# Moving the second block's activation tiles to other start addresses in SBUF

## What is computed

```python
hn = rms_norm(h, norm_mix_g)
u, gb_in, gc_in, v_in, ga_lin, gbr_lin = split(hn @ w_in)        # each 2048 wide
pooled = causal_multiscale_pool(u)                               # trailing means over 2, 4, 8, 16 tokens
y_a = einsum("blgc,gcd->blgd", pooled, pool_w) * pool_scale      # four 512 x 512 products
y_b = (gb_in * causal_depthwise_conv(gc_in * v_in, conv_w)) @ conv_out_w
g_a, g_b = split(sigmoid(concat(ga_lin, gbr_lin) + b_gate))
h = h + (g_a * y_a + g_b * y_b) @ w_o
hn = rms_norm(h, norm_ffn_g)
gate, up = split(hn @ w_gate_up)                                 # 2 x 5632 wide
h = h + (silu(gate) * up) @ w_down
out = rms_norm(h, norm_final_g)[:, 16:]
```

## Time and profile before

| | before |
|---|---|
| runs | 3424.66, 3426.06, 3426.75 us |
| profiled execution | 3418.24 us, span 3416.9 us |
| TensorE busy | 3285.0 us, 96% of the span |
| DVE, ACT, POOL busy | 48%, 40%, 5% |
| mean granted TensorE clock | 0.979 of full speed |
| second block | about 1893 to 3417 us of the span |
| moved from and to HBM | 566 MB, 166 GB/s on average |

### The profile page before, as it was taken

The page is one execution under the profiler, slowest core; times in us unless marked ns, Lnnn a source line. Parts: engine busy times, 40 slices in busy tenths (PEclk is TensorE's granted clock), DMA queues, the critical chain, the costliest instruction groups (busy, mean ns, idle before and its releaser), DMA issues.

```text
span 3416.9 us, 52152 instructions
## 1 busy us (share of the span) xinstructions
PE 3285.0 (96%) x21958; PEld 2848.6 (83%) x21958; DVE 1654.4 (48%) x2688; ACT 1360.5 (40%) x2179; POOL 173.0 (5%) x252
## 2 busy tenths in 40 slices
PE   6899999978999999999899999999999999999998
PEld 2588888863458879887459999999999999999998
DVE  1322233364663353355585675565555654555444
ACT  2322232344442254333454443344444444444343
POOL 3001000011001101000201000000000000000000
PEclk8999999989999989999899999999999999999999
DMA  8633222227644256433425455555555455555554
GB/s 308 246 123 120 93 93 97 80 76 257 237 170 154 93 185 204 142 130 115 157 77 200 160 180 185 185 179 191 186 186 188 168 187 185 187 189 186 186 187 153
DMA packets 152826, 566.09 MB, mean 166 GB/s; under 512 B 17520, under 2 KB 17648, under 8 KB 151440
## 3 DMA queue, kind: packets, MB, share of 16 engines
q1 hardware_dynamic: 146160, 529.52, 44.9%
q0 software_dynamic: 6432, 33.23, 2.7%
HBM read 550.10 MB, written 12.58 MB: 165 GB/s over the span
## 4 chain that ended last, share of the span: by engine, by line
PE 90%; DMA 4%; DVE 3%; ACT 1%; issue 1%; POOL 0%; SPq 0%; DVEq 0%; ACTq 0%; POOLq 0%
PE ps L748 20%; PE ps L750 20%; PE ps L749 20%; PE ps L737 7%; PE ps L739 7%; PE ps L738 7%; DMA sb_raw<-in_stream 4%; PE ps L658 3%; PE ps L870 1%; PE ps L856 1%; PE ps L833 1%; PE ps L849 1%; PE ps L824 1%; PE ps L665 1%; PE ps L781 1%
## 5 line engine op out<-in xcount | busy, mean ns | idle before, releaser
L1292 DVE TENSOR_TENSOR sb_wlo<-sb_raw,sb_whi 128x1024 fp32r<-128x1024 f32 (+1 forms) x814 | 993.0, 1221 | 1355.8 <-ACT sb_whi L942 1354.5
L942 ACT ACTIVATE sb_whi<-sb_raw 128x1024 fp32r<-128x1024 f32 (+1 forms) x818 | 859.5, 1051 | 1128.6 <-PE ps L750 885.5
L748 PE MATMUL ps<-sb_hn_hi,sb_whi 128*128 128x256 f32 (+4 forms) x2944 | 829.2, 282 | 4.1 <-DVE sb_hn_lo L1364 4.1
L749 PE MATMUL ps<-sb_hn_lo,sb_whi 128*128 128x256 f32 (+4 forms) x2944 | 828.2, 281 | 0.0
L750 PE MATMUL ps<-sb_hn_hi,sb_wlo 128*128 128x256 f32 (+4 forms) x2944 | 827.2, 281 | 0.0
L748 PEld LDWEIGHTS ps<-sb_hn_hi,sb_whi 128*128 128x128 f32 x2944 | 555.9, 189 | 5.2 <-DVE sb_hn_lo L1364 4.5
L750 PEld LDWEIGHTS ps<-sb_hn_hi,sb_wlo 128*128 128x128 f32 x2944 | 556.1, 189 | 0.0
L749 PEld LDWEIGHTS ps<-sb_hn_lo,sb_whi 128*128 128x128 f32 x2944 | 556.0, 189 | 0.0
L739 PE MATMUL ps<-sb_whi,sb_lo 128*128 128x512 f32 (+1 forms) x968 | 373.9, 386 | 0.0
L737 PE MATMUL ps<-sb_whi,sb_hi 128*128 128x512 f32 x896 | 353.8, 395 | 0.0
L738 PE MATMUL ps<-sb_wlo,sb_hi 128*128 128x512 f32 x896 | 349.0, 390 | 0.0
(11 more groups left out here) (265 smaller groups left out, 4030.9 us busy)
## 6 DMA issues: line engine op xcount, KB each, us to landing
sb_raw<-in_stream SPq DMA_DIRECT2D x992, 512.0 KB, 3.4
sb_raw<-in_stream SPq DMA_DIRECT2D x18, 384.0 KB, 3.0
sb_T<-in_x POOLq DMA_DIRECT2D x1, 4096.0 KB, 17.8
z_scratch<-sb_scr POOLq DMA_DIRECT2D x16, 256.0 KB, 2.5
sb_zb<-z_scratch POOLq DMA_DIRECT2D x16, 256.0 KB, 3.0
sb_bias<-in_bias POOLq DMA_DIRECT2D x4, 1024.0 KB, 10.1
x_scratch<-sb_T POOLq DMA_DIRECT2D x1, 4096.0 KB, 15.3
sb_T<-in_x POOLq DMA_DIRECT2D x2, 1536.0 KB, 7.6
```

Of the source, the lines that this page charges most:

```text
L748: PE.matmul(o, whi[:, s, w], xh, start=k == 0, stop=False)
L749: PE.matmul(o, whi[:, s, w], xl, start=False, stop=False)
L942: AC.activation(whi[:, s, 0:width], raw[:, r, 0:width], ACT.Copy).then_inc(*hi.up((g.id, c)))
L1292: VE.tensor_tensor(wlo[:, s, 0:width], raw[:, r, 0:width], whi[:, s, 0:width].bitcast(F32), ALU.subtract).then_inc(*lo.up((g.id, c)))
```

## The change

The second block's activation tiles move. Their common start goes from `block` (64 modulo 256) to the next address that is 0 modulo 256, byte 71424. Their k-tiles become 256 columns (1024 bytes) instead of 272, so that each k-tile begins at 0 modulo 256. Only the normalised input, which has to hold the 16 meta tokens too, gets 320 columns (1280 bytes); its 272 tokens are put at the end of the 320, so that a window of the last 256 begins at column 64, byte 256. The windows of 258, 260, 264 and 272 columns begin at 248, 240, 224 and 192 modulo 256. The meta tokens' tail, the residual `res`, stays where it was.

Two lines that align `raw` and `block` to 64 modulo 256 are new; both stand there already, so they move nothing: `raw`, `whi`, `wlo` and all tiles of the first block keep their addresses. No instruction is added, removed, widened or put elsewhere in any engine's order; the same instructions wait for the same semaphores, with other addresses.

```diff
--- before.py
+++ after.py
@@ -22,6 +22,8 @@
 SW = 128
 META = 16
 N2 = META + L
+NS = L + HD
+WEIGHTS_AT, ONE_AT, TWO_AT = 64, 64, 0
 FFN = 5632
 FT = FFN // P
 WINDOWS = (2, 4, 8, 16)
@@ -450,11 +452,13 @@
     rq = own("rq", [P, 4, 4])
     sk = own("sk", [P, 4])
     rope = own("rope", [P, 4, 2, 2 * HD])
+    place[0] += (WEIGHTS_AT - place[0]) % 256
     raw = own("raw", [P, RAW, CH])
     whi = own("whi", [P, RING, CH], F32R)
     whi_f = sb("whi_f", [P, RING, CH], F32, place[0] - 4 * RING * CH)
     wlo = own("wlo", [P, RING, CH], F32R)
     TB = 2048
+    place[0] += (ONE_AT - place[0]) % 256
     block = region(16 * TB * 2 + 32 * TB + 1024 + 12 * TB)
     HB = 16 * TB
     HH = sb("hi", [P, DT, 512], F32R, block)
@@ -477,27 +481,28 @@
     PTC = sb("ptc", [P, 2, 2, 256], F32, s_at + 8 * TB)
     ZB = sb("zb", [P, 2, 512], F32, s_at + 10 * TB)
 
-    NB = DT * N2 * 4
-    PH = sb("pooled_hi", [P, DT, N2], F32R, block)
-    PL = sb("pooled_lo", [P, DT, N2], F32R, block + NB)
-    CHI = sb("conv_hi", [P, DT, N2], F32R, block + 2 * NB)
-    CLO = sb("conv_lo", [P, DT, N2], F32R, block + 3 * NB)
-    YA = sb("ya", [P, DT, N2], F32, block + 4 * NB)
-    G4 = sb("g4", [P, 4, N2], F32, block + 5 * NB)
-    FH = sb("ffn_hi", [P, FT, N2], F32R, block)
-    FL = sb("ffn_lo", [P, FT, N2], F32R, block + FT * N2 * 4)
-    hn_at = block + 2 * FT * N2 * 4
-    NH = sb("hn_hi", [P, DT, N2], F32R, hn_at)
-    NL = sb("hn_lo", [P, DT, N2], F32R, hn_at + NB)
-    t3_at = hn_at + 2 * NB
-    res_at = block + 153600 - NB
-    assert t3_at + 4 * N2 * 4 <= res_at and block + 5 * NB + 4 * (N2 + 2) * 4 <= hn_at
+    LB = DT * L * 4
+    two_at = block + (TWO_AT - block) % 256
+    PH = sb("pooled_hi", [P, DT, L], F32R, two_at)
+    PL = sb("pooled_lo", [P, DT, L], F32R, two_at + LB)
+    CHI = sb("conv_hi", [P, DT, L], F32R, two_at + 2 * LB)
+    CLO = sb("conv_lo", [P, DT, L], F32R, two_at + 3 * LB)
+    YA = sb("ya", [P, DT, L], F32, two_at + 4 * LB)
+    G4 = sb("g4", [P, 4, L], F32, two_at + 5 * LB)
+    FH = sb("ffn_hi", [P, FT, L], F32R, two_at)
+    FL = sb("ffn_lo", [P, FT, L], F32R, two_at + FT * L * 4)
+    hn_at = two_at + 2 * FT * L * 4
+    NH = sb("hn_hi", [P, DT, NS], F32R, hn_at)
+    NL = sb("hn_lo", [P, DT, NS], F32R, hn_at + DT * NS * 4)
+    t3_at = hn_at + 2 * DT * NS * 4
+    res_at = block + 153600 - DT * N2 * 4
+    assert t3_at + 4 * N2 * 4 <= res_at and two_at + 5 * LB + 4 * (N2 + 2) * 4 <= hn_at
     RES = sb("res", [P, DT, N2], F32, res_at)
-    T2 = sb("tmp2", [P, 8, N2 + 16], F32, block + 3 * NB)
+    T2 = sb("tmp2", [P, 8, N2 + 16], F32, two_at + 3 * LB)
     T3 = sb("tmp3", [P, 4, N2], F32, t3_at)
     T4 = sb("tmp4", [P, 4, N2], F32, hn_at)
     SCALED = sb("scaled", [P, DT, L], F32, hn_at + 4 * N2 * 4)
-    CV = sb("cv", [P, 4, N2 + 2], F32, block + 5 * NB)
+    CV = sb("cv", [P, 4, N2 + 2], F32, two_at + 5 * LB)
     PS = nc.alloc_psum_tensor("ps", [P, 8, 512], F32)
 
     def C(name, rows=P):
@@ -554,8 +559,7 @@
         if g.x == "ckv":
             return ckv_parts(k)
         if g.x in ("hn", "latent"):
-            a = 0 if g.kind == "ffn" else N2 - g.n
-            return NH[:, k, a:a + g.n], NL[:, k, a:a + g.n]
+            return NH[:, k, NS - g.n:], NL[:, k, NS - g.n:]
         if g.x == "pooled":
             return PH[:, 4 * g.index + k, 0:g.n], PL[:, 4 * g.index + k, 0:g.n]
         a, b = {"conv": (CHI, CLO), "mixed": (PH, PL), "ffn": (FH, FL)}[g.x]
@@ -987,7 +991,7 @@
         def make_hn(tag, k):
             n = N2 if tag == "hn_mix" else L
             AC.wait_ge(*v_ev.at("xs", tag, k))
-            AC.activation(NH[:, k, 0:n], T2[:, 4 + k % 2, 0:n], ACT.Copy).then_inc(*a_ev.up((tag, k)))
+            AC.activation(NH[:, k, NS - n:], T2[:, 4 + k % 2, 0:n], ACT.Copy).then_inc(*a_ev.up((tag, k)))
 
         def evac(g, p):
             l, gid = g.layer, g.id
@@ -1361,7 +1365,7 @@
             if k + 1 < DT:
                 scaled_hn(tag, k + 1)
             VE.wait_ge(*a_ev.at(tag, k))
-            VE.tensor_tensor(NL[:, k, 0:n], T2[:, 4 + k % 2, 0:n], NH[:, k, 0:n].bitcast(F32),
+            VE.tensor_tensor(NL[:, k, NS - n:], T2[:, 4 + k % 2, 0:n], NH[:, k, NS - n:].bitcast(F32),
                              ALU.subtract).then_inc(*v_ev.up((tag, k)))
 
         def evac(g, p):
```

## The result

The changed kernel took 3380.19 us (median of 4 executions, 3379.44 to 3390.34) against 3426.4 us (4 executions): ratio 0.988, 95% interval 0.9863 to 0.9896. The forecast was 3382. Two later series of the same kernel, each timed beside the kernel before, say less: 3393.01 against 3421.05 us (7 and 22 executions, ratio 0.9933, 0.9905 to 0.9962) and 3401.4 against 3430.79 (6 and 10 executions, 0.9922, 0.9893 to 0.9952). The gain is 28 to 46 us by the medians. By the ratios it is 23 to 41 us; they are the record's own estimates and not the quotients of the medians, and the intervals of the first two series do not even overlap. The executions of the change differ from each other more than those of before: in the three series they span 11, 38 and 28 us (3379 to 3418 over all 17), those of before 4, 14 and 21. Where that spread comes from is what most of the experiments are about.

The account below looks back on a forecast made before the run. TensorE's time per matmul was taken to bound the kernel. The 256-column matmuls save 44 us and all other terms count as 0: 3426 - 44 = 3382 us, range 3375 to 3394.

Parts of the forecast that it names:

- Step 1: Second block's 256-column matmuls: each k-step of 12 goes from 1411.8 to 1360.3 ns, 44.5 us over 864, taken as 44.
- the seven flat matmuls: The last seven of a k-step's 12 matmuls at remainder 0, averaging 113.36 ns, taken as the pitch after the change.
- wake: First five matmuls of a k-step at 0, uneven after the step at 192; none expected at a constant remainder.
- Steps 2 and 3: Second block's 258-column matmuls, and those of 260, 264 and 272: counted as 0; costs of 0.9 and 0.2 us worked out.
- Step 4: ACT and DVE write and read the same shapes at new addresses: counted as 0.
- Step 5: What is late next: weight splits and loads keep up with 2.72 us per chunk; 1 us allowed for waits at group starts.
- The first: Rival: each new k-tile costs five uneven matmuls even at the old remainder; gain only 23 us, 3403 us; 6%.
- No change: Rival: the fast state depends on more than the remainder modulo 256, gain and loss cancel; 3426 us; 4%.
- The slower one: Rival: a constant remainder locks TensorE at 120.1 ns, as at a constant 64; 26 us slower, 3452 us; 3%.
- The scatter: Runs of the kernel before were taken to lie within 2 us, so about 0.2% tells a change from none.

Follow-up runs that it names:

- two64: The changed kernel with the second block's tiles beginning at 64 instead of 0 modulo 256, the weights' remainder; 3445.5 us, ratio 1.0067 to the kernel before.
- weights0: The changed kernel with the weight rings beginning at 0 instead of 64 modulo 256; 3458.89 us, ratio 1.0106 to the kernel before.
- one0: The changed kernel with the first block's activations also at 0 instead of 64 modulo 256; 3409.07 us, ratio 0.9943 to the kernel before.

## Why the prediction was right, and where it was not

**What bounds the kernel** held: TensorE, by its pitch; ACT, DVE and the loads took the faster pace without a new bound.

**Step 1** was right in kind: where the moving operand starts, relative to the weights, decides the pitch, and the seven flat matmuls in the steps at 0 were the right ones to carry over. 113.36 ns were read and 113.33 came. That there is no wake at a constant remainder is shown too, by two64 (120.0 ns flat) and by the steps of 1.36 us. As a forecast for one execution it was too simple. I took the short pitch for *the* pitch of that pair of addresses; there are two that last. In the kernel before each step of another remainder pushes the engine out of its pattern, and within a step at 0 it was always at the short pitch after five matmuls. With one remainder throughout only pauses and changes of shape do, and between them it stays where it came to rest. The trace of before could have warned: I listed flat stretches as proof of one steady state, where all 211 had the same history. Against 44.5 us the 256-column matmuls gave 39.1 in the profiled execution. Four long-pitch blocks took 4 x 192 x 4.45 ns = 3.4 us, and longer pauses and more matmuls at half clock another 1.8 (33 pitches over 150 ns, 8.1 us together, for 25 and 5.4 us before).

**Steps 2 and 3**: +1.4 and +0.2 us; 0.9 and 0.2 were worked out and counted as 0. **Step 4**: nothing seen. **Step 5**: 1 us was allowed for pauses at the heads of groups; the largest one is now 0.8 us long, where four of 0.2 us stood.

**The rivals.** The first, a wake in every step, is refuted by 1.36 us. "No change" is refuted. The slower one named the right fact, that a constant difference locks the engine into a state, and the right price; it erred in which state goes with 0 against 64. Its pitch needs equal remainders, as two64 and weights0 show. What I missed is its milder form, 117.78 ns, which lies at the old mean of 117.6: an execution whose FFN is caught in it gains almost nothing there.

**The scatter** was taken too small. "Within 2 us of each other" rested on three executions, with the profiled one 7.8 us below their median; beside the experiments 19 executions of the kernel before lay between 3412.5 and 3431.9 us.

**The time**: 3380.2 against 3382 looks better than the reasoning was, and is in part luck. The two traces differ by 37.6 us (3418.24 to 3380.61), the medians by 46; the forecast of 44 lies between, and what brought the median near it is not in the second block. The four executions of the first series have none of the long ones, over 3400, that are 6 of the other 13. Over all three series the gain is 46, 28 and 29 us, and the range to 3394 leaves out the 3401 of the last one, on a chip where before took 3431.

On the Trainium skill's section "Step-by-step: what each phase is for" of "TensorE: Matmul & The Clock Gate", that a weight load takes nothing from the running matmul's reads: two64 and the changed kernel differ in nothing but start addresses, and their second blocks by 60 us. With operands that start at the same places relative to each other (weights0, two64) the pitches are equal to 0.01 ns. So for `float32r` operands it does matter where the one begins relative to the other, and the measurement decides. That the two reads get in each other's way would explain it; no run shows it, for none took the weight loads away.

## What to carry to other kernels

Where TensorE never waits, read its pitch from starts or counts and compare the same shape in different places; a few ns between them can be the start of the moving operand relative to the weights, modulo 256 bytes here, and the best difference is another one for 512 columns (0) than for 256 (64 either way, when the short pitch lasts). A flat stretch in a trace shows a state that lasts, not that it is the only one: before building on it, ask how the engine got there and take more than one execution. When a change widens the spread of executions, four of them can flatter it: the first series here gave 0.988, the later ones 0.9933 and 0.9922.

## What the runs showed that was not expected

- Pitch by difference of starts (moving minus stationary, modulo 256 bytes), full clock, `float32r`, 128 x 128 weights: 256 columns 120.0 ns at 0, 113.33 or 117.78 at 64 and at -64, 118.67 at 128; 512 columns 226.67 at 0, 228.89 at 64, 233.33 at -64. For 512 columns only one pitch per difference was seen, in one trace each of weights0 and one0.
- One extra matmul of 16 to 128 columns can change the pitch of the 192 or 528 matmuls of the group that follows it by 4.45 ns each, and a state once reached lasted for 6336.
- The first block, with the same code and addresses, ended between 1889 and 1910 us in twelve traces. Its 1600th matmul already starts between 399 and 413 us, so most of that scatter arises early; the cause is open.
